# A fused two-block transformer kernel: where the 128 dense chunks of the expert layer's first product are placed around its two gate tables

## The reference

```
q = (xc @ w_query).reshape(C, 8, 2, 128)
sc = einsum('thpd,hpnd->thpn', q, sub_keys)              # 8 heads x 2 halves x 128 keys
top_s, top_i = top_k(sc, 16)
cand_s = top_s[:, :, 0, :, None] + top_s[:, :, 1, None, :]
best_s, best_pos = top_k(cand_s, 16)                     # 16 experts a head, 128 slots a token
gates = softmax(best_s)
u, vv = expert_down[experts], expert_up[experts]         # 16384 experts x 1024
act = gelu(einsum('cd,chkd->chk', xc, u))
out = einsum('chk,chkd->cd', gates * act, vv)
```

## Time and profile before

| quantity | value |
| --- | --- |
| time, median of 3 runs | 1520.49 us (1516.82 to 1522.25) |
| profiled execution: its own time | 1521.15 us |
| profiled execution: span of the trace | 1519.4 us |
| mean granted TensorE clock, of full | 0.983 |
| PE busy | 1409.4 us (93%) |
| DVE busy | 992.2 us (65%) |
| ACT busy | 635.2 us (42%) |
| POOL busy | 206.8 us (14%) |
| DMA queue of SP (q1) | 238.93 MB |
| DMA queue of the gathers (q0) | 67.12 MB |

### The profile page before, as it was taken

How to read it: one execution, slowest core, us unless ns; L and a number is a source line. 1 busy time by engine, 2 the same in 40 slices (tenths; PEclk the granted TensorE clock), 3 DMA queues, 4 the chain that set the end, 5 groups by cost and what they waited for, 6 DMA issues and landing times. The chain is left out here.

```text
span 1519.4 us, 24796 instructions
## 1 busy us (share of the span) xinstructions
PE 1409.4 (93%) x8327; PEld 1208.3 (80%) x8327; DVE 992.2 (65%) x2325; ACT 635.2 (42%) x1256; POOL 206.8 (14%) x170
## 2 busy tenths in 40 slices
PE   7998999987997657999999999999999999989998
PEld 4665699877996657777777777789999999659994
DVE  4666589994887658666767666665555555356761
ACT  2433251003970005533333333356665665326651
POOL 0000176442457520000000000000000000000000
PEclk9999999999999888999999999999999999999999
DMA  8330198998899991465666565484544443236620
GB/s 299 134 136 1 43 339 320 385 408 328 301 353 403 409 399 58 139 185 188 187 185 191 182 191 183 136 270 156 180 150 153 152 152 111 91 90 195 182 89 28
DMA packets 145527, 307.17 MB, mean 202 GB/s; under 512 B 39968, under 2 KB 89632, under 8 KB 143904
## 3 DMA queue, kind: packets, MB, share of 16 engines
q1 hardware_dynamic: 127008, 238.93, 47.2%
q0 software_dynamic: 18432, 67.12, 11.6%
HBM read 304.73 MB, written 1.29 MB: 201 GB/s over the span
## 5 line engine op out<-in xcount | busy, mean ns | idle before, releaser
L1333 PE MATMUL plain_u<-whole,ring 128*128 128x128 f32 x1824 | 232.1, 286 | 46.2 <-DMA ring<-in_downT 42.6
L1333 PEld LDWEIGHTS plain_u<-whole,ring 128*128 128x128 f32 x1824 | 219.8, 199 | 56.5 <-DMA ring<-in_downT 52.2
L1890 ACT ACTIVATE hT_high<-ring 128x1024 fp32r<-128x1024 f32 x128 | 135.7, 1061 | 222.3 <-PE experts_acc L249 221.2
L247 PE MATMUL experts_acc<-hT_high,experts_wh 128*128 128x512 f32 x512 | 203.2, 397 | 1.5 <-DVE hT_low L1906 1.5
L249 PE MATMUL experts_acc<-hT_high,experts_wl 128*128 128x512 f32 x512 | 202.5, 396 | 0.0
L248 PE MATMUL experts_acc<-hT_low,experts_wh 128*128 128x512 f32 x512 | 202.3, 395 | 0.0
L1462 POOL DMA_INDIRECT table<-in_down_rows,select_expert x128 | 161.8, 1264 | 155.0 <-DVE select_u L1685 118.0
L1685 DVE CUSTOM_DVE_ANT_0 table<-table,h_row 128x1024 f32<-128x1024 f32 x128 | 152.6, 1223 | 40.0 <-DMA table<-in_down_rows,select_expert 36.9
L1906 DVE TENSOR_TENSOR hT_low<-ring,hT_high 128x1024 fp32r<-128x1024 f32 x128 | 156.9, 1226 | 27.4 <-ACT hT_high L1890 27.4
L247 PE MATMUL mix_a_pj<-mix_a_wh,hT_high 128*128 128x384 f32 x368 | 129.1, 351 | 0.0
L247 PEld LDWEIGHTS experts_acc<-hT_high,experts_wh 128*128 128x128 f32 x512 | 96.0, 188 | 35.1 <-issue 7.6
(11 more groups left out here) (393 smaller groups left out, 2575.6 us busy)
## 6 DMA issues: line engine op xcount, KB each, us to landing
ring<-in_up SPq DMA_DIRECT2D x128, 512.0 KB, 3.5
ring<-in_downT SPq DMA_DIRECT2D x114, 512.0 KB
mix_raw<-in_wa SPq DMA_DIRECT2D x46, 768.0 KB, 6.1
block_w_raw<-in_w SPq DMA_DIRECT2D x16, 768.0 KB, 6.2
mix_raw<-in_wb SPq DMA_DIRECT2D x16, 768.0 KB, 6.8
ring<-in_route SPq DMA_DIRECT2D x16, 576.0 KB, 4.2
table<-in_downT SPq DMA_DIRECT2D x14, 512.0 KB, 5.3
wo<-in_wo SPq DMA_DIRECT2D x4, 1024.0 KB, 8.2
```

Source lines behind the costliest of these rows:

```text
L247: pe.matmul(out, lhs[0], rhs[0], start=start, stop=False, skip_group_check=True)
L1333: mm = pe.matmul(self.u[g % 2][:, i * P:(i + 1) * P], rows[:, k, :], self.h[:, k, P:SEQ], start=k == 0, stop=k == KD - 1, skip_group_check ...
L1890: act.activation(uh[b % 2], raw_u[b], ACT.Copy).then_inc(u_high, 1)
```

## The change

Three constants and one rule of placement are altered. `AHEAD` goes from 60 to 52: PE comes to the transposes of the slots after 52 chunks. `BESIDE` stays, so `beside` now spreads 28 chunks (52 to 79) over the 16 groups of the second table: one, or in 12 of 16 groups two. `TAIL` goes from 8 to 0: chunks 80 to 127, 48 of them, follow in one run, and the first table's groups have none between. VectorE's dot products beside the second table go from 1 + g % 2 to 2 + (g % 5 < 2) a group: 42 instead of 25, so that 80 have begun after it. The remaining 48 are made in twelve rounds of four with a join each. SP's pacing follows from the same constants.

```diff
-AHEAD = 60
+AHEAD = 52
 BESIDE = 32
-TAIL = 8
+TAIL = 0
...
+def beside_group(g):
+
+    return 2 + (g % 5 < 2)
...
-    begun = DOTS_SEARCH + sum(1 + g % 2 for g in range(GROUPS + 1))
+    begun = DOTS_SEARCH + sum(beside_group(g) for g in range(GROUPS + 1))
...
             for g in range(GROUPS):
                 spread(1, g)
-                if g % 2 == 1:
+                if g % 2 == 1 and g // 2 < TAIL:
                     chunks.project(pe, NKEYS - TAIL + g // 2)
...
-                if g % 8 == 7:
+                if g % 8 == 7 and g // 2 < TAIL:
                     chunks.gelu(act, (NKEYS - TAIL) // 4 + g // 8, tail_gelu[g // 8])
...
-                at = dots(at, 1 + g % 2)
+                at = dots(at, beside_group(g))
...
-            for g in range(2):
+            for g in range(TAIL // 4):
                 join(last + g, tail_gelu[g])
```

## The result

The changed kernel takes 1505.36 us (median of 4 runs, 1503.3 to 1506.04), the kernel before 1521.0 beside it (median of 4, 1516.82 to 1522.25). The ratio is 0.990, with a 95% interval of 0.9878 to 0.9921: 15.6 us faster, where 19.0 were forecast. The forecast was 1501.5 with a range of 1495 to 1514. A later set of four runs of the same code gave 1504.62 (1501.07 to 1505.47), a ratio of 0.9887 (0.9839 to 0.9936).

What follows compares the result with a forecast made beforehand. Transfers at 409 GB/s were taken to bound the stretch changed. An earlier first table (12.5 us) and a shorter one (6.5) gave 19.0 us: 1502.2 on the profiled execution, 1501.5 as median, range 1495 to 1514.

Steps and rivals of the forecast that it cites:

- The bound: Up to the first table, transfers at 409 GB/s bind; the lower rate between 367 and 460 us is demand, lacking 23.1 us.
- Rival (b): Second table's stage: the low rate is a limit, not a demand; 1519 us at 340 GB/s, 1512 at 358; chance 0.10.
- The transposes: Slot transposes go at 347.5 us, after 52 chunks end at 347.1 and DVE's gates at 347.4; no later wait is added.
- rival (e): The change doesn't do what it says: transposes wait for DVE; 347.4 against 347.1 leaves 0.3 us; no chance given.
- The groups: Second table's 16 groups take 5.2 us each, bounds 4.95 and 6.2, and the stage ends at about 441 us.
- (a): Second table's groups stretch to 6 us as PE and DVE wait in turn: 9.6 us less gain, 1511 us; chance 0.15.
- (d): Slower: dot products stop overlapping PE in the second table, 7.8 us a group, 1539 us; decides from 6.6; chance 0.08.
- What is not filled: Transfer idle time left around the transposes and the joins after the second table: 5 us, bounds 2 and 12.
- TAIL = 0 before the gate: Four more chunks must land ahead of the first table: 5.1 us of transfers, plus 0.5 us for the last chunk's way.
- The gate: First table starts 12.5 us earlier, at 565.4 us: 23.1 - 5.1 - 5 - 0.5.
- The first table: Without its eight chunks the first table is 6.5 us shorter, bounds 4.5 and 8; ACT's rounds then take 7.8 us.
- Rival (c): First table isn't shorter, ACT's rounds taking all: only 12.5 us gained, 1508 us; chance 0.07.

Runs made afterwards that it cites:

- the repeated one: The changed kernel run again unaltered, on the same chip as the two kernels with loads held back: 1504.62 us, ratio 0.9887 to the kernel before.
- the four chunks between and TAIL = 4: Changed kernel with chunks 52 to 55 projected between transposes and second table, chunks 124 to 127 back in the first table: 1499.23 us, ratio 0.9861.
- TAIL = 4, held, with four chunks between: Changed kernel, four chunks before the second table's first group, four back in the first table, their loads waiting for all 128 dot products: 1496.98 us, ratio 0.9841.
- TAIL = 4 with and without the hold: Changed kernel with four chunks back in the first table: 1504.27 us; with their loads also waiting for all 128 dot products: 1501.0 us.

## Why the prediction was right, point by point

**The bound.** Right: fewer bytes with the same instructions bring the first table 21 us forward, and the rate of the second table's stage was a demand and no limit: the changed kernel runs it at 401 to 409 GB/s. Rival (b) is out. The Trainium skill's rule of about 358 GB/s for transfers from HBM (DMA: Bandwidth & Descriptors, "Where 436 GB/s comes from") would have given its 1512; the trace has 409 GB/s for 161 us on end. The Trainium skill's page "HBM Reference" ("Specifications (TRN2)") says that this figure is the share with both cores of a pair streaming, and that a core alone measures well above it; with one core at work here, the trace agrees with that page.

**The transposes.** Forecast 347.5, and the last ones went at 349.3. PE was there in time, its 52 chunks were done at 344.05; DVE had the gates only at 349.03 (348.54 and its 0.49), 1.6 us later than in the execution of before. So the transposes did wait for DVE (2.37 us at the first, 0.95 at the gates), as rival (e) has it, but the price is small: the second table starts at 357.47 instead of 355.9. The end of the search differs from execution to execution, at 347.4 before, 348.9 in the repeated one and 353.4 with the four chunks between and TAIL = 4; why is not shown.

**The groups.** Forecast 5.2 us each with bounds of 4.95 and 6.2. Measured (436.63 - 357.47) / 16 = 4.95, the lower bound. PE's waits inside the stage are 1.0 us for all 16 groups. DVE waits 5.8 us for ACT's copies before merges, half of the 11.9 of before, and PE's 1.0 us shows that its one-hots are far enough ahead. Rivals (a) and (d), which need 6 and 6.6 us a group, are out.

**What is not filled.** Forecast 5 us. The windows give (409 - 372) x 13 + (409 - 247) x 12 + (409 - 401) x 17 over 409 = 6.3 us. The mechanism is the one named, the buffers run full at the transposes and open again with the first copy; the merge that follows that copy stands at 365.06, and its wait of 2.76 us is in the row. The joins after the table, for which I had put 1 to 2 us, cost nothing: 409 GB/s from 441 to 460 us. The size of this term is one execution's; the repeated one has 3.7 us.

**TAIL = 0 before the gate.** This term was mis-sized: it had 5.1 us of transfers and 0.5 for the last chunk's way, together 5.6. Between the changed kernel and the same with TAIL = 8 the last dot product moves by 556.70 - 552.13 = 4.6 us, but the join behind it by 561.03 - 553.28 = 7.7. The difference, 3.1, is DVE's wait for the last chunk's gelu (3.09 in the row): the last two chunks go back to back from 556.39 (x32) to 560.2, while the last gather has landed by 556.70. I had taken an average over the two orders of arrival; the trace has the dearer one, and with two chunks in a row. With TAIL = 0 alone the gate came 7.0 us later, there with the gather as the last piece and no such wait. 5.1 of it are the four chunks; for the other 1.9 the trace offers a cause that the term leaves out, the four loads of the experts' weights beside the last gathers, but no run shows its size. In the changed kernel these loads can have cost little on the chain that ends last: PE's last wait for a chunk is 0.47 us, and from 556.39 on PE works without a gap.

**The gate.** Forecast 12.5 us earlier, measured 12.0. The term above is 2.1 us too small and the unfilled one 1.3, which makes 3.4. What made up for most of it is not a step of the sum: from 200 to 289 us, in code that the change doesn't touch, this execution moved more than that of before, ((331 - 327) x 60 + (382 - 361) x 29) / 409 = 2.1 us. The other kernels have 356 to 391 GB/s from 260 to 289 us, so it is a difference of executions and of none of the parts. The repeated execution had 0.6 us less than that of before up to 289 us ((311 - 327) x 60 + (386 - 361) x 29, over 409) and the smaller hole of 3.7, and its first table starts at the same 565.92: in these two executions what was missing before 289 us came back in the hole. That the forecast was met within 0.5 us is in part luck, with errors that cancel. Some 0.8 us in the one and 0.9 in the other stay open.

**The first table.** Forecast 6.5 us shorter, measured 5.8. The middle came as worked out: 603.14 - 579.76 = 23.38 against 25.74, and the rounds are 7.79 us long (587.56 - 579.76 = 7.80, forecast 7.8). The end gave 2.1 (7.6 against 9.7; forecast 2.2). The head gave 1.3 instead of 2.0: from the first group to the sixth 13.84 against 15.16. The chunk's 1.8 us between groups 1 and 2 are gained, but the second group itself takes 2.70 us and took 2.24 before: the granted clock is 0.50 in the first group both times (565.92 to 569.50, 577.90 to 581.50), and in the second one 0.71 here and 0.87 there. That is 0.5 us of the 0.7; the rest is the bit of ACT's wait that I had added. Rival (c) is out.

**The parts together.** In us below the kernel before, each against the kernel before on its own chip (its median there is 1516.24 for the first four rows, 1521.0 and 1518.91 for the changed kernel, 1518.91 for the last), and where its first table and its experts start in the trace:

| kernel | us below before | first table | experts |
| --- | --- | --- | --- |
| TAIL = 0 alone | -2.6 | 584.85 | 629.87 |
| AHEAD = 52 alone | -0.5 | 575.11 | 626.35 |
| dot products alone | 9.8 | 564.81 | 614.91 |
| AHEAD and dot products | 15.1 | 558.32 | 608.48 |
| the changed kernel | 15.6, 14.3 | 565.92 | 610.75 |
| TAIL = 4, held, with four chunks between | 21.9 | 558.06 | 604.67 |

The forecast had given TAIL = 0 a gain of 6.5 - 5.6 = 0.9 us; the traces say 7.6 - 5.3 = 2.3 lost (with the other parts) and 1.4 lost (alone), and the times can't tell it from nothing. Its sign was wrong at a size that hardly shows. The mechanism held: the transfers are the bound, and the 42 dot products feed them. In the traces, 12.0 + 5.8 = 17.8 of the 19.0 us arrived. The medians show 15.6, since the profiled execution of the changed kernel lies 2.1 us below the median of its four, where I had converted with the 0.66 of the one before.

## What to carry to other kernels

When the transfer rate sinks in a stage without any engine at its limit, work out what the stage frees per step (buffers of each stream, times their size, over the step's time): if that equals the rate seen, the rate is a demand, and moving consumers of the scarcer buffers into the stage fills it. Moving the producer's or the matmul's work earlier without such a consumer only moves the hole: here it was worth nothing alone and 5 us together with the consumers. Moving a piece of work from behind a gate to before it must be priced by the way of the last piece through every engine up to the gate, not by its bytes alone, and with what the next phase loads into the buffers that it frees.

## What the runs showed of the hardware

- **The transfers.** One core held 408 to 409 GB/s, at a DMA share of 1.03, from two queues (chunks from SP, gathers of 128 rows of 4 KB from POOL) for 161 us on end, 389 to 550 us, while PE was up to 100% busy, DVE 98% and ACT 90% in parts of the same stretch. No engine's load showed in the rate.
- **TensorE's clock at the experts' start.** In four kernels (AHEAD = 52 alone, TAIL = 4 with and without the hold, and held with four chunks between) the experts' first matmul ran at the lower of the two levels, 1.2 GHz. PE in order of time in the last of these, with the six short matmuls that stand before the experts in each kernel:

```profile
602.24 0.91 PE L258 MATMUL experts_idle<-ident 128*128 128x128 f32 x6 [1.37 <-PEq L1397]
604.67 0.77 PE L250 MATMUL experts_acc<-hT_high,experts_wh 128*128 128x512 f32 x1 [1.53 <-DVE hT_low L1920]
```

Its windows before and after that point:

```profile
602.00:604.67 2.67, 0.91 (x6) 0.77 (x7) 2.09 (x4) 2.00 (x2) 0.00 (x0) 0.87 0.00 0
604.67:607.00 2.33, 2.33 (x6) 1.85 (x7) 1.62 (x3) 0.00 (x0) 0.00 (x0) 0.50 0.49 121
```

And those of the changed kernel before its experts:

```profile
605.00:608.00 3.00, 1.95 (x18) 1.76 (x16) 0.00 (x0) 2.04 (x2) 0.00 (x0) 1.00 0.00 0
608.00:610.75 2.75, 0.91 (x6) 0.77 (x7) 2.09 (x4) 2.02 (x3) 0.00 (x0) 1.00 0.00 0
```

PE did the same right before both starts, 0.91 us of matmuls in the last 2.7 us, and in the 3 us before that it was busy 1.87 us here and 1.95 there. The granted clock fell in the one (0.87, then 0.50) and stayed at 1.00 in the other. In the first 10 us of the experts this kernel makes 31 matmul records and the changed one 43: at 45 in 10 us this is 2.7 us, and the rest of its span is 2.6 us longer (893.4 against 890.8). So a good part of what it had gained by then, 6.1 us, is lost again in this execution. What decides there was not tried.
